# Identity multiplications in TensorE's waits in a two-block transformer kernel

## What is computed

```python
def first_block(...):
    px = split(modulate(rms_norm(x, norm1), sh1, sc1) @ w_in)      # q k v | hq zf zb i g
    na_x = neighbourhood_attention(px[0], px[1], px[2], k_ctx, v_ctx, na_rpb)
    hg_x = hgrn2_mixer(px[3:], pc[3:], lb, hg_norm)
    x = x + gt1 * (concatenate([na_x, hg_x]) @ w_out)
    x = x + gt2 * peer_ffn(modulate(rms_norm(x, norm2), sh2, sc2), peer_wq, peer_keys, peer_u, peer_v)
    return rms_norm(x, norm_f)

def second_block(x, ...):
    for l in range(2):
        m = even_mixer(x) if l == 0 else odd_mixer(x)   # retention + stick-breaking; differential
        x = layer_norm(ALPHA * x + m, ln1_g[l], ln1_b[l])
        x = layer_norm(ALPHA * x + conv_ffn(x), ln2_g[l], ln2_b[l])
    return x
```

## Time and profile before

| | |
|---|---|
| three runs | 3709.18, 3736.78, 3744.82 us; median 3736.78 us |
| the profiled execution | 3727.29 us, of which the span from the first to the last instruction is 3725.5 us |
| granted clock, mean over the span | 0.932 |
| TensorE's longest waits by releaser | the gathered rows' diagonals 328.6 us in 238 waits; splits of activations after norms 42.8 us in 6 |

### The profile page before, as it was taken

How to read it: one execution, slowest core, us unless ns; L and a number is a source line. 1 busy time by engine, 2 the same in 40 slices (tenths; PEclk the granted TensorE clock), 3 DMA queues, 4 the chain that set the end, 5 groups by cost and what they waited for, 6 DMA issues and landing times. The chain is left out here.

```text
span 3725.5 us, 34772 instructions
## 1 busy us (share of the span) xinstructions
PE 3191.9 (86%) x12250; PEld 2170.3 (58%) x12250; DVE 2095.0 (56%) x3738; ACT 838.7 (23%) x2134; POOL 704.9 (19%) x679
## 2 busy tenths in 40 slices
PE   7999888797777777777777799889999999999998
PEld 6887678683232222232222267467887787678876
DVE  1322577467785764784444463255874454558753
ACT  2112323122222222222222220231220102312101
POOL 0001344004344443444333320000000000100000
PEclk7999888898999999999999999579999997699999
DMA  6657888668999999999999922002332231023322
GB/s 213 203 202 254 286 281 255 214 215 363 421 421 421 419 412 421 419 410 421 421 416 419 397 83 90 6 1 74 96 96 91 81 107 33 1 64 97 99 86 73
DMA packets 154291, 845.76 MB, mean 227 GB/s; under 512 B 15328, under 2 KB 15584, under 8 KB 87584
## 3 DMA queue, kind: packets, MB, share of 16 engines
q0 software_dynamic: 83392, 578.06, 38.1%
q1 hardware_dynamic: 70752, 265.79, 22.3%
HBM read 841.70 MB, written 136.31 MB: 263 GB/s over the span
## 5 line engine op out<-in xcount | busy, mean ns | idle before, releaser
L753 PE MATMUL PS<-AR,HC 128*128 128x512 f32 x1536 | 728.2, 619 | 254.8 <-ACT HC L1198 251.9
L199 PE MATMUL PS<-AR_r,RHI 128*128 128x512 f32 x1888 | 758.8, 402 | 75.6 <-DVE AR_r L1369 42.8
L201 PE MATMUL PS<-AR_r,RING_r 128*128 128x512 f32 x1888 | 743.2, 394 | 0.0
L753 PEld LDWEIGHTS PS<-AR,HC 128*128 128x128 f32 x1536 | 283.7, 194 | 698.4 <-ACT HC L1198 398.2
L1547 DVE SCALAR_TENSOR_TENSOR AR<-AR 128x1024 f32<-128x1024 f32 x384 | 470.1, 1225 | 364.9 <-DMA AR<-peer_uv,XC 363.1
L200 PE MATMUL PS<-AR_r,RHI 128*128 128x512 f32 x1504 | 592.4, 394 | 0.0
L458 POOL DMA_INDIRECT AR<-peer_uv,XC x384 | 398.8, 1038 | 739.9 <-PE PS L753 546.5
L199 PEld LDWEIGHTS PS<-AR_r,RHI 128*128 128x128 f32 x1888 | 360.5, 191 | 162.3 <-issue 66.8
L1351 DVE CAST RHI<-RING 128x1024 fp32r<-128x1024 f32 x256 | 178.7, 698 | 472.1 <-DMA RING<-in_wstream 469.0
L201 PEld LDWEIGHTS PS<-AR_r,RING_r 128*128 128x128 f32 x1888 | 359.6, 190 | 76.6
L200 PEld LDWEIGHTS PS<-AR_r,RHI 128*128 128x128 f32 x1504 | 287.3, 191 | 64.3 <-issue 6.0
(11 more groups left out here) (328 smaller groups left out, 3681.3 us busy)
## 6 DMA issues: line engine op xcount, KB each, us to landing
RING<-in_wstream SPq DMA_DIRECT2D x304, 512.0 KB, 3.6
peer_uv<-in_peer_u SPq DMA_DIRECT2D x48, 1024.0 KB, 11.9
peer_uv<-in_peer_v SPq DMA_DIRECT2D x48, 1024.0 KB, 12.7
peer_uv<-in_peer_v POOLq DMA_DIRECT2D x16, 1024.0 KB, 20.9
peer_uv<-in_peer_u POOLq DMA_DIRECT2D x16, 1024.0 KB, 21.2
AR<-peer_uv,XC POOLq DMA_INDIRECT x384
XL<-in_xl SPq DMA_DIRECT2D x1, 2048.0 KB, 10.0
RHI_f<-peer_uv,XC POOLq DMA_INDIRECT x128
```

The costliest lines, as they stand in the source:

```text
L199: pe.matmul(out, sh, mh, start=start, stop=False)
L201: return pe.matmul(out, sl, mh, start=False, stop=stop)
L753: mm = pe.matmul(bank(2 * (tt % 2) + x), DIAG[:, n % NDIAG, :], ROWS_UV[n % NROW][:, D + 512 * x:D + 512 * x + 512], start=(j == 0), stop= ...
```

## The change

A helper `keep_clock(b, n)` on TensorE issues n fp32r matmuls with the identity as stationary operand and the identity, repeated four times, as the moving one: 512 columns into PSUM bank b. No one reads that bank before it is started anew. They signal nothing. The calls stand at 21 places in TensorE's program (one of them in the loop over two directions, one in `ffn`, which runs twice, two in the first steps of a loop) and make 318 matmuls. The heads of stick-breaking attention get one block after the first scores and none in the others. DVE's copy of the identity into `IDN_R` moves from behind the first modulation to the start of its program and signals `eye_ready`, and TensorE waits for it once, behind `passing(pe, 1)`. Ahead of barrier 15 TensorE also waits until four of the `dv` tiles are evacuated.

```diff
-        v_turned = sem("v_turned")
+        v_turned, eye_ready = sem("v_turned"), sem("eye_ready")
...
+            eyes = IDN_R[:].unsqueeze(1).to_broadcast([P, 4, P])
+            def keep_clock(b, n):
+                for _ in range(n):
+                    pe.matmul(bank(b), IDN_R[:], eyes, start=True, stop=True)
...
             passing(pe, 1)
+            pe.wait_ge(eye_ready, 1)
+            keep_clock(6, 16)
...
             tiles(FIRST["g"], 4, H1S, "h1", main, free, b)
+            keep_clock(7, 8)
             barrier(pe, 2)
...
                     na_scores(i)
+                if i < 2:
+                    keep_clock(7, 4)
...
                     if x % 2 == 1:
                         modulate(1)
+                keep_clock(6, 24)
                 after(pe, s, "kd", 1, 1)
...
             barrier(pe, 6)
+            keep_clock(1, 24)
             tiles(FIRST["out"], KT, MIXS, "mix1", main, n2, follow=rms(n2))
             passing(pe, 7)
+            keep_clock(5, 22)
...
             passing(pe, 9)
+            keep_clock(5, 13)
...
+            keep_clock(7, 8)
             barrier(pe, 10)
...
+            keep_clock(0, 12)
             barrier(pe, 11)
...
                     sb_scores(h + 1)
+                if h == 0:
+                    keep_clock(7, 18)
...
             barrier(pe, 12)
+            keep_clock(5, 28)
...
             passing(pe, 13)
+            keep_clock(5, 15)
...
                         weights_up(pe, u, c0, g, j)
+                keep_clock(5, 14)
                 after(pe, u, "act", 4 + FT, FT)
...
             passing(pe, 14)
+            keep_clock(5, 15)
...
+            pe.wait_ge(dv_evac, 4)
+            keep_clock(4, 8)
             barrier(pe, 15)
...
                     df_scores(i)
+                if i < 3:
+                    keep_clock(6, 6)
...
+            keep_clock(0, 6)
             for h in range(2):
                 turn_head(h)
+            keep_clock(0, 8)
             tiles(FIRST["out_o"], ...)
             passing(pe, 16)
+            keep_clock(5, 15)
...
             dve.wait_ge(s_in, 80)
+            dve.tensor_copy(IDN_R[:], IDN[:]).then_inc(eye_ready, 1)
             dve.wait_ge(n1["root"], 1)
...
-            dve.tensor_copy(IDN_R[:], IDN[:])
             first_chunks("q")
```

## The result

The changed kernel takes 3687.9 us (median of 20 runs, 3650.6 to 3706.9) against 3729.1 us for the kernel before (20 runs, 3700.4 to 3750.1): a ratio of 0.989, 95% interval 0.9862 to 0.9918, so 41 us or 1.1% faster. In every ratio here a run over 1.5% above the fastest of its kernel is left out; the medians in us hold all runs. The profiled executions differ by the same amount: 3686.6 against 3727.3 us. The prediction, 3656 us, had the direction right and the gain too large, 72 us on the profiled execution where 40.7 came. The time lies in the stated range (3628 to 3697) and outside the forecast's own (3640 to 3672).

The account below looks back on a forecast made before the run. TensorE, busy 86% of the span and often at half clock, was taken as the bound. Gains of 22.2 + 3.6 + 2.5 + 25.7 + 2 + 16 = 72 us gave 3655 us from 3727.3, predicted as 3656, range 3628 to 3697.

Parts of the forecast that it names:

- rival 1: Retention falls back to half clock anyway, everything else holds: 3681 us, chance 0.14.
- rival 5: Identity products do not raise or hold the clock, so blocks overhang their waits: slower, 3769 us, chance 0.08.
- rival 3: All low steps of differential attention go: up to 22 us more gained, 3636 us, chance 0.10.
- Ten starts, 22.2 us: Ten projection starts at half clock behind waits, 47.3 us low, recovered at 0.47 of their length: 22.2 us gained.
- what stays is under the shortest that cost anything: At the projection starts: waits left behind the blocks, 0.4 to 2.0 us, are too short to bring a low stretch.
- Neighbourhood attention, -4.7: Its first four steps, 14.97 us at mean granted 0.54, shrink to 10.2 us: gain 4.7, net 3.6 us.
- SP's queue and its row copies move with TensorE: Chunks are asked for as used, so row copies follow TensorE; the gathered rows' stage keeps its length.
- Recurrence, 2.5: At full clock the transposes lose only ACT's 0.26 us wait for TensorE, six times: 1.25 us per direction, 2.5 together.
- Retention, 25.7: Eight products ahead of barrier 10 fill the wait, so retention's 54.61 us at half clock run full: 25.7 us gained.
- Differential attention, 16: First ten steps, 48.77 us run low, speed up: 13.1 us from six steps and 2.9 from the first four, together 16.
- Rival 2: Differential attention falls back to the low clock in its first head: 3671 us, chance 0.12.
- Rival 4: Only the ramps are regained, neither long stretch in retention nor differential attention: 3697 us, chance 0.08.

Follow-up runs that it names:

- e5_half_rows: The changed kernel with all 318 added products on 64 rows of the identity in place of 128: 3717.7 us, ratio 0.9952 to the kernel before.
- e2_all_but_barrier10: The changed kernel without its block of eight products ahead of barrier 10, the other 20 places kept: 3721.5 us, ratio 0.9923 to the kernel before.
- e8_barrier10_out_again: The changed kernel without its block ahead of barrier 10, run once more unchanged for a second profile: retention took 67.98 us.
- e12_fewer_in_diff_attention: The changed kernel with 12 row copies moved to SP's queue and 16 further products in differential attention: 3641.0 us, ratio 0.9726 to the kernel before.

## Why the prediction was right or wrong, point by point

- *The sum*: the number nearest to the result is rival 1's 3681 us, whose mechanism (retention falls back) did not occur in the profiled execution. Two slips of arithmetic matter little: the waits in rival 5 sum to 95.9 us, not 95 (3768 us), and 22 us under 3655 is 3633, not rival 3's 3636.
- *The identity raises and holds the clock*: right; the clock went from 0.50 to 1.00 4.2 us into the block ahead of q and 6.2 us into the one ahead of `out`, and in the profiled execution q, wq, rq, out_e, both `up`, the first `down` and dq start at 1.00, and rival 5 (3769 us) is out. It rose with nearly all operands zeros. With 64 rows in place of 128 the same two blocks, 7.2 and 10.60 us long, stayed at 0.50 (e5_half_rows).
- *Ten starts, 22.2 us*: the mechanism was right, the term too large: 14.7 us in the trace, 13 by the ratio of the run with them alone. The step that failed is "what stays is under the shortest that cost anything": the earlier start let TensorE meet a chunk and an evacuation that it had met later before (dq to dv, 1.4 us longer instead of shorter), and the 2.37 us that it waited there brought a low stretch. The prediction's own list of signs of error had this one ("waiting for chunks or splits where it now works densely"), but no price for it. Of the 7.5 us that are missing, dq to dv make 4.3 (2.8 expected, 1.4 lost), the second `down` 1.6 (its low stretch stays) and rq to sv 1.0. Behind the 1.8 us of waiting that stay ahead of `down` the clock fell in twelve of twenty cases, so such a wait is not too short to cost anything; behind the 0.5 to 1.4 us that stay ahead of wq, rq, out_e, both `up`, dq and out_o it fell in none.
- *Barrier 2, +1.1*: right, 1.2 us. *Neighbourhood attention, -4.7*: 4.5 us in the trace, but here, too, the trace was a lucky one. Of nine executions with full-row blocks there, three had no low time in the stage (103.6 us), three had 3.4 us (104.4 to 105.2), and three had 10.2 us and took 107.5 to 108.4, close to the 108.1 before.
- *"SP's queue and its row copies move with TensorE"*: this step failed. GpSimd's 32 copies do not. Barrier 3 waited for them before the change too, and the earlier trace rows left out the 10.34 us there because it was no wait behind a norm. The net 3.3 us of the stage, and more, were given back. The reading that would have caught it: the timeline names GpSimd's sequencer as releaser and GpSimd has had nothing to do for 22.9 us.
- *Recurrence, 2.5*: 3.9 us, 1.9 to 2.0 in each direction. It was mis-sized low. The transposes alone gained more than that: they took 5.4 and 5.1 us before and 2.8 twice in the changed kernel, and the rest of the stage lost 0.9. The prediction kept ACT's six evacuations at 0.60 us each; at full clock ACT does the six in 3.04 us, 0.51 each and without the gaps.
- *`out`, 0; stick-breaking, 2*: both as measured. That the latter agrees to a tenth is luck: it had bounds of -2 and +5, and the heads took 93.6 to 95.8 us in eight executions with full-row blocks ahead of them and none inside, 97.6 to 98.7 in four without.
- *Retention, 25.7*: 25.5 us in this execution. But the reason given, that neighbourhood attention holds the clock with 64-row scores, was only half of it. Without the block it also held in one execution of five, so the block is worth 26 to 29 us in the executions that would have fallen, four of the five seen, and nothing in the others.
- *Differential attention, 16*: this term failed. That the first ten steps could be had was right (33.5 us in one execution). The later low stretches "may shift but I count them as before" is the step that failed. They move forward, and the first one grows: before, they began 72.6 and 123.8 us into the stage and lasted 27.3 us each; in the changed kernel they began at 50.0 and 91.0 us and lasted 34.1 and 27.3, with three falls of 6.8 us beside them. The low time went from 102.3 to 81.6 us only, and the added products cost a part of that. Rival 2's number, 3671 us, was nearer to the result than the forecast, but its mechanism happened in part only: the clock did fall in the first head, 2.2 us into the stage, and rose again 6.8 us later. Of the 38 us that the prediction gave as the upper bound 32 were really there (151.1 to 118.7 us), for 16 more products in the right places.
- *Rival 4*, only the ramps: they gave 14.7 of 3727 us in the trace, 0.4%, where its 3697 us had 30 for all but the two long stretches. The measured 3687.9 us is close to its number, but by other terms than its own: retention's 25.5 us, and the 28 us to be had in differential attention, lay in dense work.

## What to carry to other kernels

Here filling TensorE's waits paid where TensorE set the pace behind them (14.7 us at ten starts, 25.5 us in retention), and not ahead of barrier 3, where it waited for GpSimd's copies: 4.5 us won, 6.4 us more of waiting. Ask first, for each stage, what its barrier really waits for, and look at transfers of the queue that is drained as well as at instructions. Low stretches inside dense work were worth more here (25.5 us in retention, 28 us in differential attention) than those at starts (14.7 us). In differential attention blocks at the stage's start didn't cure them (154.1 us mean with them, 153.7 without), while 16 full-row products spread over the whole stage left 10.2 us low (118.7 us). Where the clock falls in some executions and not in others, as in retention without its block (in four of five), one profile of each kernel tells little on a stage; collect the stage's length over all executions before giving it a price.

## What the runs showed of the hardware that had not been expected

- Without the block ahead of barrier 10 the same program, behind the same wait of 2.19 us, had retention at granted clock 1.00 in one execution (e2_all_but_barrier10, 39.25 us) and at 0.50 for 61.4 us in another (e8_barrier10_out_again, 67.98 us).
- 24 products of 64 rows and 512 columns, 10.60 us without a break ahead of `out`, ran at 0.50 throughout (e5_half_rows, 684.50:695.10). The 24 of 128 rows at the same place, 8.65 us, ran at 0.50 for 6.2 us and then at 1.00 (the changed kernel, 670.27:678.92). Of fifteen blocks of 64 rows that began at 1.00, twelve kept it while they ran (2.1 to 5.3 us), and behind six of these it fell within 1.8 us.
- In the changed kernel the clock fell in differential attention with TensorE 93% busy in the 7 us before (3110.00:3117.00), and in the 34.0 us behind that, 100% busy, it stayed at 0.50. With 16 full-row products more in the whole stage 10.2 us of 118.7 were low (e12_fewer_in_diff_attention), in place of 81.6 of 148.7.
- GpSimd stood 29.3 us at its drain without an instruction of its own in the changed kernel, while the transfers of its queue (q0, `software_dynamic`) were under way. In eleven executions TensorE went on 1.44 or 1.45 us after the last of 32 copies had landed, and in the three with 12 of them taken out of that queue the barrier opened 0.43 us behind TensorE's last product, 22.7 to 27.2 us after the last copy.
